# The order of ScalarE's copies at the seams of the MLP in a two-layer RWKV and differential-attention trunk

## The reference, cut to what matters

```python
x = x + mixer(rmsnorm(x, g0)) @ w_o
x = x + square(relu(rmsnorm(x, g1) @ w1)) @ w2      # w1 1024 x 4096, w2 4096 x 1024
x = x + (p_i @ w_up) * sigmoid(rmsnorm(x, g2) @ w_gate)   # w_up 256 x 1024
```

## Time and profile before

| | |
|---|---|
| median of 3 runs | 1458.83 us (1457.23 to 1460.25) |
| profiled execution, span | 1461.9 us |
| PE busy | 1388.5 us, 95% of the span |
| DVE, ACT, POOL busy | 703.3, 618.7, 543.1 us |
| mean granted PE clock | 0.987 |

### The profile page before, as it was taken

The page is one execution under the profiler, slowest core; times in us unless marked ns, Lnnn a source line. Parts: engine busy times, 40 slices in busy tenths (PEclk is TensorE's granted clock), DMA queues, the critical chain, the costliest instruction groups (busy, mean ns, idle before and its releaser), DMA issues.

```text
span 1461.9 us, 23258 instructions
## 1 busy us (share of the span) xinstructions
PE 1388.5 (95%) x9043; PEld 1161.7 (79%) x9043; DVE 703.3 (48%) x1116; ACT 618.7 (42%) x924; POOL 543.1 (37%) x311
## 2 busy tenths in 40 slices
PE   6999998789999999999999999999999999999998
PEld 5767887775878888888878787766878888888877
DVE  6899987658354200432148463277453201341153
ACT  7885626455433221333254442486342212232352
POOL 3121012214533544344442244345435443535432
PEclk9999999999999999999999999999999999999999
DMA  6222200301223333323223422200222333232321
GB/s 198 77 67 79 66 1 3 125 4 58 87 87 115 99 116 99 103 87 112 90 95 116 145 87 87 87 1 30 87 87 86 115 118 98 87 115 87 114 87 58
DMA packets 119900, 126.43 MB, mean 86 GB/s; under 512 B 6268, under 2 KB 114556, under 8 KB 119816
## 3 DMA queue, kind: packets, MB, share of 16 engines
q1 hardware_dynamic: 119120, 123.99, 26.0%
q0 software_dynamic: 320, 0.66, 0.2%
q10 hardware_dynamic: 376, 0.61, 0.2%
HBM read 123.12 MB, written 2.12 MB: 86 GB/s over the span
## 4 chain that ended last, share of the span: by engine, by line
PE 72%; DVE 11%; ACT 7%; issue 7%; POOL 2%; ACTq 0%; POOLq 0%; DVEq 0%
PE pb L634 20%; PE pb L636 19%; PE pb L635 19%; ACT whi L1485 3%; DVE xl L2464 2%; POOL wlo L528 2%; PE pb L1358 1%; PE pb L764 1%; PE pb L1326 1%; PE pb L1328 1%; PE pb L1327 1%; PE pb L1385 1%; DVE xl L2118 1%; PE pb L1367 1%; ACT KV L1733 1%
## 5 line engine op out<-in xcount | busy, mean ns | idle before, releaser
L525 POOL TENSOR_TENSOR wlo<-wraw,whi 128x1024 fp32r<-128x1024 f32 x96 | 227.8, 2373 | 655.5 <-ACT whi L1485 496.4
L634 PE MATMUL pb<-xh,whi 128*128 128x512 f32 x1088 | 421.1, 387 | 11.3 <-POOL wlo L528 5.9
L636 PE MATMUL pb<-xh,wlo 128*128 128x512 f32 x1088 | 414.5, 381 | 0.0
L635 PE MATMUL pb<-xl,whi 128*128 128x512 f32 x1088 | 414.3, 381 | 0.0
L1485 ACT ACTIVATE whi<-wraw 128x2048 fp32r<-128x2048 f32 x108 | 206.3, 1910 | 225.0 <-PE pb L636 222.0
L634 PEld LDWEIGHTS pb<-xh,whi 128*128 128x128 f32 x1088 | 206.9, 190 | 63.5 <-issue 23.0
L528 POOL TENSOR_TENSOR wlo<-wraw,whi 128x1024 fp32r<-128x1024 f32 x96 | 232.9, 2426 | 0.0
L636 PEld LDWEIGHTS pb<-xh,wlo 128*128 128x128 f32 x1088 | 206.8, 190 | 29.4
L635 PEld LDWEIGHTS pb<-xl,whi 128*128 128x128 f32 x1088 | 207.1, 190 | 28.5 <-issue 1.0
L634 PE MATMUL pb<-hid_h,whi 128*128 128x512 f32 x512 | 194.9, 381 | 2.1 <-POOL wlo L528 2.1
L635 PE MATMUL pb<-hid_l,whi 128*128 128x512 f32 x512 | 194.2, 379 | 0.0
(11 more groups left out here) (324 smaller groups left out, 1808.4 us busy)
## 6 DMA issues: line engine op xcount, KB each, us to landing
wraw<-in_mlp_w_dram SPq DMA_DIRECT2D x128, 512.0 KB, 4.3
wraw<-in_rwkv_w_rkvo_dram SPq DMA_DIRECT2D x32, 512.0 KB, 4.4
wraw<-in_ple_w_gate_dram SPq DMA_DIRECT2D x16, 512.0 KB, 4.4
xtok<-in_x_dram SPq DMA_DIRECT2D x8, 512.0 KB, 6.1
wraw<-in_diff_w_q_dram SPq DMA_DIRECT2D x8, 512.0 KB, 4.0
wraw<-in_w_k_shared_dram SPq DMA_DIRECT2D x8, 512.0 KB, 4.4
wraw<-in_w_v_shared_dram SPq DMA_DIRECT2D x8, 512.0 KB, 4.3
wraw<-in_diff_w_o_dram SPq DMA_DIRECT2D x8, 512.0 KB, 3.9
```

The lines of the kernel that those rows point to most:

```text
L525: pool.tensor_tensor(wlo[:, par, front], wraw[:, par, front], whi[:, par, front].bitcast(F32), ALU.subtract)
L634: mm(o, wh, ah, start=first, stop=False)
L635: mm(o, wh, al, start=False, stop=False)
L636: return mm(o, wl, ah, start=False, stop=last)
```

## The change

ACT's list is reordered at the four seams, and one instruction of PE's list is moved.

- Seam A: `high` of the MLP's second block goes ahead of the last two splits.
- Seams B and C: `high` of the second product's second block goes ahead of the last two `hid_h` copies. The last turn of the loop is written out for that.
- Seam D: `high` of the first gate block goes ahead of the last two splits, and the first two `UP` copies go ahead of the last two squares.
- Seam D on PE: `norm_total` goes ahead of tile 7 instead of tile 6.

No work is added or removed.

```diff
 def ple(...):  # PE
-                    if m == 6:
+                    if m == 7:
                         norm_total(4)
...
 def proj(...):  # ACT
                         splits(gain, 8 * (n0 + 3), 0, 6)
+                        high(n0 + 5, (n0 + 5) % 2)
                         act.wait_ge(s.dense_v, ev0 + 8)
                         splits(gain, 8 * (n0 + 3), 6)
...
+            def up_copy(n, m):
+
+                act.wait_ge(s.pe_step, 8 * n + m + 1)
+                A(UP[:, m, :], pb[m % 4][:, :], ACT.Copy).then_inc(s.dense_a, 1)
...
-                    def two_blocks(i, first):
+                    def two_blocks(i, first, last=False):
                         opening = first and half == 0
                         for h in range(2):
-                            if not (opening and h == 1):
+                            if not opening:
                                 high(m0 + 2 * i + h + 1, (m0 + h + 1) % 2)
...
+                            if last and h == 1:
+                                high(m0 + 9, (m0 + 1) % 2)
...
-                    with act.Fori(1, 4) as i:
+                    with act.Fori(1, 3) as i:
                         two_blocks(i, False)
+                    two_blocks(3, False, True)
...
-                        with act.Fori(0, 4) as i:
+                        high(m0 + 2, m0 % 2)
+                        with act.Fori(1, 4) as i:
...
                         for b in range(8):
-                            high(m0 + b + 1, (m0 + b + 1) % 2)
+                            if b:
+                                high(m0 + b + 1, (m0 + b + 1) % 2)
                             if b == 7:
                                 splits(gain, None, 0, 6)
+                                high(m0 + 9, (m0 + 1) % 2)
                                 act.wait_ge(s.dense_v, ev0 + 48)
                                 splits(gain, None, 6)
+                                up_copy(m0 + 8, 0)
+                                up_copy(m0 + 8, 1)
...
             def ple(layer, n, ni):
-                high(n + 1, (n + 1) % 2)
...
-                for m in range(CT):
-                    act.wait_ge(s.pe_step, 8 * n + m + 1)
-                    A(UP[:, m, :], pb[m % 4][:, :], ACT.Copy).then_inc(s.dense_a, 1)
+                for m in range(2, CT):
+                    up_copy(n, m)
```

## The result

The changed kernel takes 1447.05 us (median of 4 runs, 1446.3 to 1448.24), the kernel before 1458.77 us: 11.7 us less, a ratio of 0.9921 (95% interval 0.9907 to 0.9935). The forecast was 1448.0.

The account below looks back on a forecast made before the run. PE, busy 95% of the 1461.9 us span, was taken as the bound. Seams give 1.4 + 0.21 + 1.17 + 1.6 = 4.4 us per layer, 8.8 in two; 1461.9 - 8.8 - 5.1 (clock stretches) = 1448.0 us, 8-in-10 range 1443.5 to 1454.

Parts of the forecast that it names:

- The eight gaps: PE's idle gaps at seams A to D in two layers: 2 x (2.61 + 0.21 + 1.17 + 2.43) = 12.8 us.
- A new stall of 1.2 us: Seam A: PE waits 1.2 us for the sum of squares at `norm_total`, replacing 2.61; net -1.4 us per layer.
- I keep 1.2: Seam A: DVE's low part gets in between POOL's two instructions, as in the trace, so the stall is 1.2 us.
- the letter of the rule: Seam A: POOL's second instruction, issued 0.02 us ahead of DVE's low part, goes first; stall 1.4 instead of 1.2 us.
- the late `hid_l`: Seams B and C: DVE's last `hid_l` tiles finish about 4 us later, near 500.5; PE reads them from 509.8, so hidden.
- 0.8 us predicted: Seam D: PE stalls 0.8 us for `norm_total`'s sum ahead of tile 7, replacing 2.43; net -1.6 us per layer.
- the 3.1 us between the profiled execution and the median: Profiled 1461.9 us against the median, read as one to three fewer half-speed stretches, so 1448.0 holds for the median too.
- all three stretches: Half-clock periods of PE behind seam A of layer 0 and seam D of both layers: 1.7 us each, 5.1 together, gone.
- the half-speed stretches stay: Rival on PE's clock behind the seams: only 8.8 us gained, 1453.1 from the profiled run, 1450.0 from the median; chance 0.22.
- DVE and POOL don't hinder each other: Rival at the seams: no `norm_total` stall, 4.0 us more gained, 1444.0 us; chance 0.10.
- the wait moves whole: Rival at seams A and D: `norm_total` as late as the old wait, only B and C gain 2.8 us, 1456.0; chance 0.10.
- the slower rival: Rival at seams A and D: four short new stalls each draw a long half-speed stretch, 13.6 us lost, 1461.6; chance 0.03.

Follow-up runs that it names:

- the experiment: The changed kernel with the sum's product (`norm_total`) back ahead of tile 6 at seam D: 1449.28 us, 1.9 more than the changed kernel beside it.
- fillers: The kernel before, with five small matmuls of constants into an unused bank ahead of each PE wait at seams A and D: 1456.95 us, ratio 0.9974.

## Why the prediction was right

**The bound and the gaps.** The eight gaps were sized right (12.8 predicted, 12.7 counted) and all went.

**Seam A.** A new stall of 1.2 us was predicted, 1.2 and 1.3 measured, but by another way than I laid out. I let DVE's low part in between POOL's two instructions, since the trace had shown that. In fact POOL's second went first: DVE's last two low parts took 2.9 and 0.8 us, not 0.8 and 2.9, and PE stood still at step 6 as well. The step that failed is "I keep 1.2" over the letter of the rule: what counts is which of the two instructions was issued first. In the block before, DVE's had been waiting since POOL's first instruction, and so it is at seam D, where DVE did get in between; at seam A it came 0.06 us behind POOL's second. That the first issued takes the way and the other waits is what the Trainium skill says ("SBUF — State Buffer", section "Who interferes with whom"), and the trace agrees with it at all of these places. The prediction had worked out that letter beside its own: step 6 late by 0.5 us and 1.4 in all, where 0.4 to 0.5 and 1.2 to 1.3 were measured. The price was right because DVE's last low part ended at about the same time either way.

**Seams B and C.** As predicted: the load was there, the copies weren't delayed, and the late `hid_l` was hidden.

**Seam D.** 0.8 us predicted, 0.7 measured. That it would have been 2.1 ahead of tile 6 was predicted; the experiment had 1.9.

**The clock.** The mechanism held: no stretch stands behind a seam any more, and with fillers in the old stalls the time fell too. The size was right in part by luck. The prediction took the 3.1 us between the profiled execution and the median as stretches that the median hadn't, which left 5.1 - 3.1 = 2.0 us to be gained from the median; 2.9 were, and the fillers gained 3.0. But that 3.1 compared a span with a time. The execution was 5.3 us above the median, more than all three stretches are worth. By the prediction's own reading nothing would have been left to gain there, and the forecast would have been 1464.1 - 8.8 - 5.1 = 1450.2, 3.1 above what was measured. What is wrong is the reading that this excess is stretches at the seams: half-speed time outside them alone varies from 18.9 to 29.9 us between profiles, which is 5.5 us of the span. That error of 3.1 us and the 2.2 us left out of the span nearly cancelled. Worked out from the medians, 1458.8 - 8.8 - 3.0 gives 1447.0.

**The rivals.** That the half-speed stretches stay (1450.0 from the median) is out by the windows and by the median. That DVE and POOL don't hinder each other is out by the profile and by the kernel in which POOL waits, and that the wait moves whole is out by its size. No short stall at the seams drew a half-speed stretch in either profile of the changed kernel, so the slower rival is out too.

## What to carry to other kernels

In a list that one engine works off in order, look at what stands ready behind a waiting instruction: when the wait is long enough to hold it, moving it forward is free on that engine. Then ask what it sets going elsewhere, since here POOL's earlier start slowed DVE's chain and a third of the gain went into the next wait; moving the reader of that chain later got most of it back. And where one profile shows clock stretches, don't take their number as a fixed part of the time: it differs from one execution to the next, and the medians of kernels with and without the stalls say what they cost. Before a profile's span is compared with a run's time, find out by how much the two differ for one and the same execution.

## What the runs showed of the hardware

- Of a DVE instruction with two SBUF inputs and a POOL instruction that reads SBUF, the first issued goes first even where they come 0.03 and 0.06 us apart: DVE's, the later one, took 2.9 us instead of 0.9. A DVE instruction that came during the first of two POOL instructions got in ahead of the second, which took 2.94 us instead of 2.36. With POOL held back, both of DVE's took 1.78 us again.
- The old PE stalls at seams A and D, 2.3 to 2.7 us from start to start, were followed by 3.4 us at half the clock in 8 of 12 cases over four profiles, and by full clock in the others. The two of 2.3 and 2.1 us with POOL held back, the two of 1.9 us with the sum's product ahead of tile 6, and those of 1.3 us and less at the seams were followed by none. Matmuls of constants in the stall kept the full clock in 4 of 4.
- The half-speed time outside the seams was 18.9 to 29.9 us in twelve profiles of nearly the same program.
- A run's time was 2.2 us above its span.
